# Up projections of two feed-forward blocks: the last 16 column blocks of each layer as seven half-size products instead of eight, with weight sums made by DMA in DRAM

## What is computed

```python
def conv_ffn(h, w_up, conv_w, conv_b, w_down):      # h: 512 x 1024, w_up: 1024 x 5632, w_down: 2816 x 1024
    a, gate = jnp.split(h @ w_up, 2, axis=-1)
    a = lax.conv_general_dilated(a, conv_w[:, None, :], window_strides=(1,), padding=[(CONV_W - 1, 0)],
                                 dimension_numbers=('NWC', 'WIO', 'NWC'), feature_group_count=D_FF) + conv_b
    return (jax.nn.silu(a) * gate) @ w_down         # CONV_W = 3, depthwise, over the tokens

for i in range(2):
    x = x + attention_i(rms_norm(x, attn_norm[i]))
    x = x + conv_ffn(rms_norm(x, ffn_norm[i]), ffn_w_up[i], ffn_conv_w[i], ffn_conv_b[i], ffn_w_down[i])
return rms_norm(x, final_norm)
```

## Time and profile before

| | |
|---|---|
| median of 3 runs | 1130.2 us (1130.11 to 1130.2) |
| the profiled execution's own time | 1129.55 us |
| its span in the trace | 1127.8 us |
| PE busy | 1116.1 us of the span |
| DVE busy | 718.6 us |
| ACT busy | 477.1 us |
| POOL busy | 3.2 us |
| DMA | 101.98 MB, mean 90 GB/s |

### The profile page before, as it was taken

The page is one execution under the profiler, slowest core; times in us unless marked ns, Lnnn a source line. Parts: engine busy times, 40 slices in busy tenths (PEclk is TensorE's granted clock), DMA queues, the critical chain, the costliest instruction groups (busy, mean ns, idle before and its releaser), DMA issues.

```text
span 1127.8 us, 15482 instructions
## 1 busy us (share of the span) xinstructions
PE 1116.1 (99%) x5544; PEld 957.1 (85%) x5544; DVE 718.6 (64%) x1240; ACT 477.1 (42%) x954; POOL 3.2 (0%) x20
## 2 busy tenths in 40 slices
PE   8999999999999999999999999999999999999997
PEld 8999888888888888888999999788888888888886
...
PEclk9999999999999999999999999999999999999999
...
GB/s 207 102 63 51 1 150 112 74 112 85 101 109 77 74 75 95 104 99 168 113 56 58 56 59 55 4 129 111 112 75 111 97 89 112 57 75 93 93 102 103
DMA packets 144862, 101.98 MB, mean 90 GB/s; under 512 B 12121, under 2 KB 137270, under 8 KB 144822
## 3 DMA queue, kind: packets, MB, share of 16 engines
...
...
## 4 chain that ended last, share of the span: by engine, by line
PE 93%; DVE 4%; ACT 1%; issue 1%; DMA 0%; SPq 0%; DVEq 0%
PE ps L590 24%; PE ps L591 24%; PE ps L592 23%; PE ps L666 16%; PE ps L707 2%; PE ps L889 2%; PE ps L908 1%; PE ps L768 1%; DVE w_lo L1685 0%; DMA x_tok<-in_x 0%; DVE h_lo L1717 0%; ACT w_hi L1213 0%; DVE xT L2049 0%; DVE x_tok L2276 0%; DVE ssacc L1710 0%
## 5 line engine op out<-in xcount | busy, mean ns | idle before, releaser
L1213 ACT ACTIVATE w_hi<-raw 128x512 fp32r<-128x512 f32 (+2 forms) x204 | 192.1, 969 | 295.4 <-PE ps L592 292.8
L590 PE MATMUL ps<-h_hi,w_lo 128*128 128x512 f32 x704 | 274.3, 390 | 0.0
L591 PE MATMUL ps<-h_lo,w_hi 128*128 128x512 f32 x704 | 274.3, 390 | 0.0
L592 PE MATMUL ps<-h_hi,w_hi 128*128 128x512 f32 x704 | 274.3, 390 | 0.0
L1685 DVE TENSOR_TENSOR w_lo<-raw,w_hi 128x512 fp32r<-128x512 f32 (+2 forms) x204 | 222.8, 1114 | 16.6 <-ACT w_hi L1213 16.4
L590 PEld LDWEIGHTS ps<-h_hi,w_lo 128*128 128x128 f32 x704 | 132.2, 188 | 27.7 <-issue 0.3
L591 PEld LDWEIGHTS ps<-h_lo,w_hi 128*128 128x128 f32 x704 | 132.2, 188 | 27.5
L592 PEld LDWEIGHTS ps<-h_hi,w_hi 128*128 128x128 f32 x704 | 132.2, 188 | 27.3
L2087 DVE TENSOR_TENSOR normed<-ps,rstd 128x512 f32<-128x512 f32 x44 | 30.4, 692 | 160.5 <-PE ps L592 155.0
L666 PE MATMUL ps<-w_hi,h_lo 128*128 128x384 f32 x368 | 126.3, 343 | 0.2
L666 PE MATMUL ps<-w_hi,h_hi 128*128 128x384 f32 x368 | 125.9, 342 | 0.0
...
## 6 DMA issues: line engine op xcount, KB each, us to landing
raw<-in_ffn_w_up SPq DMA_DIRECT2D x88, 512.0 KB, 4.6
raw<-in_ffn_w_down SPq DMA_DIRECT2D x44, 512.0 KB, 3.2
raw<-in_b_w_in SPq DMA_DIRECT2D x24, 512.0 KB, 4.7
...
raw<-in_a_w_in SPq DMA_DIRECT2D x8, 256.0 KB, 7.1
out<-x_tok SPq DMA_DIRECT2D x8, 256.0 KB, 2.0
```

The lines of the kernel that those rows point to most:

```text
L590: pe.matmul(out_, a_lo, b_hi, start=start, stop=False)
L591: pe.matmul(out_, a_hi, b_lo, start=False, stop=False)
L592: return pe.matmul(out_, a_hi, b_hi, start=False, stop=stop)
L1213: act.activation(w_hi[:, s, at], raw[:, s, at], ACT.Copy).then_inc(hi_done, 1)
```

## The change

For the last 16 blocks of both layers (`PLAIN = (6, 6)`: six stay as they were) the block's product is treated as two by two quarters: the features in halves 1 and 2 of 4 chunks each (rows of the weights), the tokens in halves of 256, and the columns as `a` and `gate`. The eight quarter products become seven of 4 chunks x 3 = 12 matmuls with 256 tokens each (84 matmuls of 128 x 256). With A and G for the columns of `a` and `gate`, the weights that they need beside the given ones are S1 = G1 + G2, S3 = A1 + G1, S2 = A1 + S1 and S4 = A2 + S2, and on the token side T1, T3, T2, T4, differences of quarters of the normed activations.

The weight sums don't depend on the activations. POOL makes them by DMA in DRAM from the program's start on (`weight_sums`): per group of 128 rows by 1024 columns four copies of 512 KB, then four accumulating DMAs of 512 KB, with waits between. There are 8 groups for layer 0 and after them 8 for layer 1. SP's loads for block 6 of a layer wait until that layer's groups are done. A block's load is then 1.5 MB into `raw` and 0.25 MB (S4) into a new single buffer.

During the six plain blocks DVE also makes the normed activations (`normed_h`) and their differences (`t_source`), and ACT and DVE split them into seven pairs of operands (`op_high`, `op_low`), of which four lie where `h_hi` and `h_lo` were and can only be written as the last plain block leaves those. The output of seven products is put together by five additions out of PSUM (`outputs`) and one copy by ACT (`m1_from`); the first tap of the convolution moves to ACT (`first_tap`); the two multiplications with `rstd` go away.

```diff
+PLAIN = (6, 6)
...
+            def load_seven(l, s, f):
+                if is_block(f, PLAIN[l], PLAIN[l] + 1):
+                    sp.wait_ge(lo_done, part_done(f"up{l}", f - 2))
+                    sp.wait_ge(sum_landed, sums_in(l))
+                else:
+                    sp.wait_ge(wlo_done, nth(l, f) * 2 - 4)
+                wv = ffn_w_up[l].rearrange("(k p) n -> p k n", p=P)
+                sv = w_sums[l].rearrange("(q k p) n -> p (q k) n", p=P, k=HK)
+                rv = raw[:, s, :].rearrange("p (k n) -> p k n", n=P)
+                sp.dma_start(rv[:, 0:HK, :], wv[:, HK:KC, bass.ds(f * P + F, P)]).then_inc(raw_landed[s], 16)
+                sp.dma_start(rv[:, HK:HK + KC, :], wv[:, :, bass.ds(f * P, P)]).then_inc(raw_landed[s], 16)
+                sp.dma_start(rv[:, HK + KC:, :], sv[:, 0:3 * HK, bass.ds(f * P - PLAIN[l] * P, P)])\
+                  .then_inc(raw_landed[s], 16)
+                if is_block(f, PLAIN[l]):
+                    load_fourth(l, f)
+                elif not is_block(f, PLAIN[l] + 1):
+                    load_fourth(l, f - 1)
             def v_at(ph):
                 return D + 256 if ph == "attnA" else 2 * D
...
+            def weight_sums(l, rows, c, done):
+                wv, sums = ffn_w_up[l], w_sums[l]
+                a, gate = PLAIN[l] * P + c, PLAIN[l] * P + c + F
+                def part(half, at):
+                    return wv[half * HALF_D + rows:half * HALF_D + rows + P, at:at + SUM_COLS]
+                s1, s3, s2, s4 = (sums[q * HALF_D + rows:q * HALF_D + rows + P, c:c + SUM_COLS] for q in range(4))
+                pool.dma_start(s1, part(1, gate)).then_inc(sum_landed, 16)
+                pool.dma_start(s3, part(0, a)).then_inc(sum_landed, 16)
+                pool.dma_start(s2, part(0, a)).then_inc(sum_landed, 16)
+                pool.dma_start(s4, part(1, a)).then_inc(sum_landed, 16)
+                pool.wait_ge(sum_landed, done + 4 * 16)
+                pool.dma_start(s1, part(0, gate), accum_op=ALU.add, max_dma_last_dim=4 * SUM_COLS).then_inc(sum_landed, 16)
+                pool.dma_start(s3, part(0, gate), accum_op=ALU.add, max_dma_last_dim=4 * SUM_COLS).then_inc(sum_landed, 16)
+                pool.wait_ge(sum_landed, done + 6 * 16)
+                pool.dma_start(s2, s1, accum_op=ALU.add, max_dma_last_dim=4 * SUM_COLS).then_inc(sum_landed, 16)
+                pool.wait_ge(sum_landed, done + 7 * 16)
+                pool.dma_start(s4, s2, accum_op=ALU.add, max_dma_last_dim=4 * SUM_COLS).then_inc(sum_landed, 16)
+                pool.wait_ge(sum_landed, done + 8 * 16)
+            done = 0
+            for l in range(2):
+                for c in range(0, (FB - PLAIN[l]) * P, SUM_COLS):
+                    for rows in range(0, HALF_D, P):
+                        weight_sums(l, rows, c, done)
+                        done += 8 * 16
         @block.tensor
...
+            def product(l, f, bank, half, w_high, w_low, o):
+                if is_block(f, PLAIN[l]):
+                    pe.wait_ge(oplo_done, len(OPERANDS) * l + OPERANDS.index(o) + 1)
+                out_ = ps[:, bank, half * HT:(half + 1) * HT]
+                for kc in range(HK):
+                    c = slice(kc * P, (kc + 1) * P)
+                    ins = hi_lo(out_, w_high[:, c], w_low[:, c], op_hi[o][:, kc, :], op_lo[o][:, kc, :],
+                                start=(kc == 0), stop=(kc == HK - 1))
+                return ins
+            def seven_products(l, s, f):
+                pe.wait_ge(wlo_done, nth(l, f) * 2)
+                if is_block(f, PLAIN[l] + 1):
+                    pe.wait_ge(u_done, FB * l + PLAIN[l])
+                elif not is_block(f, PLAIN[l]):
+                    pe.wait_ge(c12_done, nth(l, f) - 2)
+                at = 4 - 4 * s
+                def part(n):
+                    return w_hi[:, s, n * QC:(n + 1) * QC], w_lo[:, s, n * QC:(n + 1) * QC]
+                product(l, f, at, 0, *part(1), "B11")
+                product(l, f, at, 1, *part(4), "T3").then_inc(first_bank, 1)
+                product(l, f, at + 1, 0, *part(2), "B21")
+                product(l, f, at + 1, 1, *part(5), "T2")
+                product(l, f, at + 2, 1, *part(3), "T1")
+                product(l, f, at + 2, 0, *part(0), "T4")
+                pe.wait_ge(s4lo_done, nth(l, f))
+                product(l, f, at + 3, 0, s4_hi[:, :], s4_lo[:, :], "B22").then_inc(products_done, 1)
             def down_pair(l, r, is_first, is_last):
...
+            def m1_from(l, s, f):
+                act.wait_ge(first_bank, nth(l, f))
+                if is_block(f, PLAIN[l]):
+                    act.wait_ge(u_done, FB * l + PLAIN[l])
+                else:
+                    act.wait_ge(c12_done, nth(l, f) - 1)
+                act.activation(m1_kept, ps[:, 4 - 4 * s, 0:HT], ACT.Copy).then_inc(m1_out, 1)
...
+            def t_source(l, n, o, plus, minus):
+                if n == 0:
+                    dve.wait_ge(oplo_done, len(OPERANDS) * l + 3)
+                else:
+                    dve.wait_ge(t_sum, 4 * l + n)
+                dve.tensor_tensor(op_source(o), op_source(plus), op_source(minus), ALU.subtract).then_inc(t_sum, 1)
...
+            def seven_low(l, s, f, half):
+                n = 3 * QC
+                at = slice(half * n, (half + 1) * n)
+                dve.wait_ge(whi_done, nth(l, f))
+                dve.tensor_tensor(w_lo[:, s, at], raw[:, s, at], w_hi[:, s, at].bitcast(F32), ALU.subtract)\
+                   .then_inc(wlo_done, 1)
...
+            def outputs(l, s, f):
+                at = 4 - 4 * s
+                dve.wait_ge(products_done, nth(l, f))
+                dve.wait_ge(m1_out, nth(l, f))
+                own.link(dve.tensor_tensor(normed_parts[:, 0:4:3, :], halves(ps[:, at + 1, :]),
+                                           m1_kept.unsqueeze(1).broadcast_to((P, 2, HT)), ALU.add))
+                own.link(dve.tensor_tensor(m1_kept, ps[:, at, HT:T], u2_kept, ALU.add))
+                dve.tensor_tensor(halves(gated[:, 0, :]), halves(ps[:, at + 2, :]),
+                                  m1_kept.unsqueeze(1).broadcast_to((P, 2, HT)), ALU.add).then_inc(c22_done, 1)
+                own.link(dve.tensor_tensor(u2_kept, ps[:, at + 3, 0:HT], u2_kept, ALU.add))
+                dve.tensor_tensor(normed[:, 0, HT:T], ps[:, at + 2, HT:T], u2_kept, ALU.add).then_inc(c12_done, 1)
...
+                gate(l, 0, p - 2)
+                seven_low(l, 0, p, 0)
+                seven_low(l, 0, p, 1)
+                op_low(l, "T3")
+                op_low(l, "T2")
+                op_low(l, "T1")
+                op_low(l, "T4")
+                gate(l, 1, p - 1)
+                fourth_low(l, p)
+                seven_low(l, 1, p + 1, 0)
+                seven_low(l, 1, p + 1, 1)
+                def seven(s, f):
+                    outputs(l, 1 - s, f - 1)
+                    fourth_low(l, f)
+                    seven_low(l, 1 - s, f + 1, 0)
+                    taps(l, f - 1)
+                    seven_low(l, 1 - s, f + 1, 1)
+                    gated_u(l, f - 1)
+                seven(1, p + 1)
+                seven(0, p + 2)
...
```

332 lines of the change are left out of this document (287 added, 45 removed).

## The result

| | before | changed |
|---|---|---|
| median | 1130.15 us | 1280.7 us (1272.1 to 1281.2, 4 runs) |
| ratio | 1 | 1.131, 95% interval 1.127 to 1.136 |
| span of the profiled execution | 1127.8 us | 1278.5 us |

The changed kernel is 13% slower, 167 us above the forecast and outside its range.

A forecast was written before the change was run, and what follows sets the result against it. The prediction took PE as the bound, busy 1116.1 of 1127.8 us. It summed 1129.6 - 31 + 5 + 1 + 6 + 3 = 1113.6, with the median 0.6 higher: 1114 us, range 1104 to 1124.

The forecast's parts named there:

- -31 us: PE's gain in 32 changed up blocks: 84 matmuls of 118 ns, 9.91 us a block, 0.97 us less each.
- +5 and +1: PE's stalls in us: at the passage into seven products (2.5 a layer), and at up's end for a bank (0.4).
- gain eaten: Rival: several small bounds together, or DVE's instructions 0.15 us dearer, cancel the gain; 1125 to 1145 us, chance 0.10.
- PE's stream doesn't shorten: Rival: 118 ns doesn't hold over 84 matmuls in a row; at 129 ns the gain is zero; chance 0.03.
- I take 24: POOL's DMAs: 24 us for a group of weight sums, copies priced once and sums twice, between 18.4 and 35.2.
- most of them fit in there: SP's own loads, 51 us of transfer until 205 us, fit into POOL's 58 us of waits, a quarter left over.
- sums needed by 215, ready at 209: Layer 0's sums: needed by 215 us for block 6, ended at 209, so no stall.
- sums late: Rival: a group takes over 24 us, so SP still waits when block 6 is due; slower, chance 0.27.
- case of 28 us with nothing hidden: Late sums at 28 us a group, SP's loads not hidden: sums end at 279, stall 64, time 1178 us.
- +6: Kernel's start: POOL's first group puts 17 us of transfer where 6 are free from 5 to 30 us; 6 us delay.
- +3, near equal shares: Layer 0's new blocks beside layer 1's sums: loads keep about half the DMA engines; 3 us lost, high bound 77.
- loads starved: Rival: sums in time, but layer 0's seven-product blocks run at up to 16.3 us; 1150 to 1188 us, chance 0.12.

The follow-up runs named there:

- bursts of 16: Changed kernel with four groups of sums a stage (16 copies, then 8, 4 and 4 sums between waits), rows 8 KB apart; 1325.2 us, ratio 1.173.
- bursts of eight: Changed kernel with two groups of sums a stage, rows 12 KB apart, chain begun late, layer 1's sums held; 1138.1 us, ratio 1.007.

## Why the prediction was wrong

**Right: the stream and its cover.** The forecast took 118 ns a matmul and -31 us; it is 120 ns and -25.6, the rounding of starts that it named (28) and a little more. DVE's 9.28 us of 9.91 came out as 9 us of 10.08, with 1.1 free; in the kernel without sums PE waits for DVE's low parts only in the two passages. These were given +5 and +1 and cost 3.0 in all (the 12 - 9.9 of the prediction is 2.1 a layer, not the 2.5 that it took; 1.4 was measured). Without sums the kernel took 1107.5 us, where these terms alone give 1130.2 - 31 + 6 = 1105. The rivals "gain eaten" and "PE's stream doesn't shorten" are refuted.

**Wrong, and the step that failed: the price of a group, "I take 24", with "most of them fit in there" for SP's loads.** Together they are 25.6 us a group (209 us for eight); measured are 40.5. The bounds of the prediction did hold it: its high price of 35.2 and nothing hidden end the sums at 337, they ended at 328. What failed is the choice between the bounds. The 24 were worked out from loads into SBUF and a store, not from a transfer of this kind. The 40.5 have three parts:
- A group with rows 12 KB apart and nearly nothing beside it takes 28.1, 4 above the value taken: 8.4 for 7.4, 8.3 for 7.4, 5.7 and 5.6 for 4.6, so each stage is about 1 us dearer. The fixed part of a stage was given 1.8 us; the two runs in which groups share their stages both saved 3.1 us for each stage less. The rule that was weighed (the Trainium skill, "Collectives: The Full Stack", "The bandwidth ceiling: the fold count and why AG ≠ RS ≠ AR") says that a reduction runs at half the rate of a copy; here, with rows 8 KB apart, two sums in a stage took 12.8 us and two copies 6.5, which agrees, while a single sum took 7.4 us and a single copy 5.0 to 5.3, which is less than twice.
- Another 8 us are the place of the sums in DRAM (35.9 for 28.1). No term stood for that. The Trainium skill has something near it: "DMA: Bandwidth & Descriptors", "Latency and other measured facts", reports that copies between HBM tensors whose rows lie 4 or 8 MiB apart run at half rate, and that 4 KiB of padding at 4 MiB restores the full one; it calls its explanation an inference. It gives nearly full rate at 512 KiB, while the runs here show a loss with rows 8 KB apart and quarters 4 MB apart. So they agree that padding helps, but the loss is smaller (10.8 us for 8.3 in the four copies), and they don't show whether rows or quarters matter. The 11.6 us for four copies that the prediction estimated from the same section lie above both layouts.
- The last 4.6 us are crowding by the program's own loads, 1.6 in the prediction: the first group took 50.0 us, the last 35.9.

From it follows the rest of "sums needed by 215, ready at 209": ready at 328. That was the rival "sums late" in its mechanism, its sign and its place (all of SP's queue, then ACT, DVE, PE); its size was cut off at 35 us a group, and its case of 28 us with nothing hidden, 1178 us, is near what the rows 12 KB apart gave (1165.7). What the sum didn't contain was that the wait asks for twice the sums that the next blocks read. It stood in the row of the diff (`sums_in(l)`), and the time at which the ninth block wants its sums was never worked out; splitting this wait brought back 90 us.

**Wrong: "+6" for the start, bounds 0 to 11.** It was +18.7, and +17.5 with the old kernel behind it. The sum counted only the transfer that fits no gap. The trace shows 10.2 us of PE without work from 5 to 30 us where it was 1.9, and a clock of 0.73 in the same stretch for 1.00. Begun at 33 or 57 us, a chain with one group a stage left the start at 163.3 to 163.5, where it is without any sums (163.4).

**Wrong: "+3, near equal shares".** It was 48.8, with 77 as the high bound: the rival "loads starved" happened too, at 3.05 us a block over 16 blocks. Holding the chain removed 45.3 of it. The waits name what is starved: most often S4's load, which has one buffer and so the least lead, 5.5 us in the middle for 256 KB. That POOL's transfers with rows of 4 KB displace SP's with rows of 512 B is what the runs show; the turns by whole packets, which the prediction took from the Trainium skill for this rival, no trace shows or refutes.

**The clock.** The granted clock is 0.52 in the stretch of the standstill, and behind it the 21 steps shown above are 213 ns instead of 120: 2 us at 1.2 GHz for 2.4. That isn't all of it: in layer 0's new blocks, where PE runs dry again and again, the clock is 0.90, and the same matmuls keep PE busy for 16 us longer, a third of the 48.8. It follows from PE's waiting, for with layer 1's sums held it is 1.00 from 350 us on, but the waits cost that much more through it, and no term of the prediction had it.

**Open:** rows or quarters, as said; how much of the 5 us of padding in layer 1 is crowding; and why bursts of 16 did so much more harm than bursts of eight (227.7 against 166.4), where the start of the chain and the layout differ as well.
